# Column sums of four-tile arrays: one strided VectorE sum and one TensorE product in place of four products

## The chip, the core and the metric

The kernel runs on one core of a Trainium2 chip, as one program. The metric is the device time of one execution in microseconds (us). TensorE multiplies matrices, VectorE and ScalarE do elementwise work, SyncE issues the loads of the weights. On the profile's pages these are PE (matmul) and PEld (weight load), DVE, ACT and SP. TensorE's granted clock is given as a share of 2.4 GHz: 1.00 is 2.4 GHz and 0.50 is 1.2 GHz, the other of its two levels.

## What is computed

256 tokens of width 2048 run through two layers of a first block and one layer of a second, all in float32. Each layer normalizes its input, multiplies it by a wide input matrix, runs several mixers on slices of the result, normalizes each mixer's output over its channels, multiplies by an output matrix, and ends in a gated feed-forward part. What matters here are the norms over the 512 channels of a mixer, whose data stand with the channels on the partitions:

```python
# first block, in each of its two layers
hf = h.astype(jnp.float32)
mu = jnp.mean(hf, axis=-1, keepdims=True)
var = jnp.mean(jnp.square(hf - mu), axis=-1, keepdims=True)
hf = (hf - mu) * lax.rsqrt(var + EPS) * ln_g + ln_b
y_a = jax.nn.silu(hf)
...
y = jnp.concatenate([rms_normalize(y_a), rms_normalize(y_b), rms_normalize(y_c)], axis=-1)
# second block, in its one layer
y_b = rms_norm(rglru_mixer(...), grp_norm_w[l, 0])
y_d = rms_norm(short_conv_mixer(...), grp_norm_w[l, 2])
```

Ten of these sums over channels are touched: in each layer of the first block the mean and the variance of the convolution branch, the squares of `y_a` and the squares of `y_c` (the pooling branch); in the second block the squares of the LRU branch and of the short convolution.

## The kernel before

An array of 512 channels by 256 tokens stands as four tiles of 128 channels (partitions) by 256 tokens, side by side in a row of 1024 numbers per partition. `column_sums` sums it over all 512 channels: for each tile one product of the constant matrix `ones` (128x128, in the tile `C`) with the tile, the four accumulated in one PSUM bank, so that each of the 128 rows of the bank holds the sum. ScalarE then takes the root of the bank into `XL[:, 0, :]` (`root_of_sums`), VectorE takes its reciprocal into `XL[:, 1, :]` and multiplies all four tiles by it. `XL` has four rows of 256; row 2 isn't in use at these places.

The large products are cut into units of 1024 weights per partition. SyncE loads a unit into `WS`, ScalarE copies its rounded part to `WH` (L749), VectorE takes what is left into `WL` (`split`, L1320), and TensorE multiplies with both (L1858, which is the line of every plain product). All three tiles are rings of four. The work of the mixers is woven in by hand: in each loop over units `u`, each engine runs its split for unit `u + 4` and the part of `mixers_pe`, `mixers_act` or `mixers_dve` (`mixers2_...` in the second block) that is written for the number `u`. Tables such as `MEAN_AT, VAR_AT, RMS_AT = 57, 59, 62` and `POOL_RMS_AT = 80`, `LRU_RMS_AT = 21`, `SC_RMS_AT = 89` say at which unit. The order on an engine is therefore fixed when the program is built, and an instruction that waits holds up everything behind it on its engine.

At `u` TensorE first multiplies unit `u` and then does its part of the mixers. VectorE does its part of the mixers first and then the split of unit `u + 4` (except in the last unit of each eight in the first block's input part). The scores of attention head `h` (L1858, `SCR` 64x128 by 64x256, from `SCORES_AT`) go from TensorE to VectorE (L970, L973), then to ScalarE's exponential (L440), then back to TensorE, which transposes them (L1642).

Semaphores of the places: `s_cv` counts the steps of the convolution (124 per layer), `s_sqr` ScalarE's arrays of squares in the first block, `s_csq` those in the second, `s_col` and `s_csum` the finished column sums.

Of the kernel before, what the change touches and what calls it, by code (L numbers as in the profile page):

```python
# [9 lines left out]
ALU = mybir.AluOpType  # L10
ACT = mybir.ActivationFunctionType
AX = mybir.AxisListType.X
# [66 lines left out]
IN_ORDER = [0, 1, 2, 4, 6, 3, 5, 7, 8]  # L79
IN_BASE = [0, 4, 2, 0, 4, 0, 4, 0, 4]  # L80
TAPS = 31

# [33 lines left out]
def build(nc, a, out, stop=None):  # L118
    with ExitStack() as ctx:
# [67 lines left out]
        f3 = lambda t: t[:, 0:1024].rearrange("p (a b) -> p a b", a=4)  # L187
        flat = lambda v: v.rearrange("p a b -> p (a b)")
        junk = [T1[:, 0:1024], T2[:, :], T3[:, :], flat(XL[:, :, :])]
        row_scale = lambda n: PR[:, 192:192 + S] if n < 2 * DEPTH else flat(ROWS[:, :, :])  # L190
        by_row = lambda n: row_scale(n)[:, None, :].to_broadcast((P, 4, S))
        SCALED = [0, 2, 4, 5]
# [756 lines left out]
        def mixers_dve(dve, l, u):  # L949
# [8 lines left out]
            def y_low(kt, high, src):  # L958
# [2 lines left out]
                dve.scalar_tensor_tensor(out=XT[:, kt, 1, :], in0=src, scalar=col(G_MIX + kt), in1=XT[:, kt, 0, :].bitcast(F32),  # L961
                                         op0=ALU.mult, op1=ALU.subtract).then_inc(s_yt, 1)

            for h in heads_at(SCORES_AT, u):
                if h == 0:
                    dve.wait_ge(s_kc, 32 * (l + 1))
                dve.wait_ge(s_S, 16 * l + h + 1)
                if h >= 2:
                    dve.wait_ge(s_p, 16 * l + h - 1)
                dve.scalar_tensor_tensor(out=neg_s[:, h % 2, :], in0=PS[:, score_bank(h), :], scalar=-1.0,  # L970
                                         in1=KC[:, K_BIAS:K_BIAS + 2 * S], op0=ALU.mult, op1=ALU.subtract).then_inc(s_sb, 1)
                dve.wait_ge(s_sb, 16 * l + h + 1)
                dve.tensor_reduce(neg_max[:, 2 * (h % 2):2 * (h % 2) + 2],  # L973
                                  neg_s[:, h % 2, :].rearrange("p (t k) -> p t k", t=NT), AX, ALU.min).then_inc(s_nm, 1)
            for h in heads_at(OUTPUT_AT, u):
                if h % 4 == 3:
# [7 lines left out]
                    dst = y_b[:, :, 256 * g:256 * g + 256].rearrange("p t (h e) -> p h t e", e=64)  # L984
                    dve.tensor_tensor(dst, o, r[:, :, :, None].to_broadcast((P, 4, NT, 64)), ALU.mult).then_inc(s_yb, 1)
            if u == MEAN_AT:

                dve.wait_ge(s_cv, 4 * TAPS * (l + 1))
                dve.wait_ge(s_col, 4 * l + 1)
                for n in range(4):  # L990
                    ins = dve.scalar_tensor_tensor(out=acc[:, n, :], in0=PS[:, 7, 0:S], scalar=-1.0 / 512, in1=acc[:, n, :],
                                                   op0=ALU.mult, op1=ALU.add)
                ins.then_inc(s_lna, 1)
# [67 lines left out]
        def mixers2_dve(dve, u):  # L1061
# [56 lines left out]
            if u == LRU_SCAN_AT:  # L1118
# [5 lines left out]
                dve.wait_ge(s_lsq, 2)  # L1124
                dve.tensor_tensor(lru_xc, lru_xc, lru_gate, ALU.mult).then_inc(s_ly, 1)
            if u == LRU_RMS_AT:
                over_root(1, lru_xc, s_cn)

            if u in (DECAY_AT, DECAY_T_AT):
# [138 lines left out]
            if u == SC_OUT_AT:  # L1268
# [4 lines left out]
                low(4, sgu_yT, lambda i: col(G2_GRP + 4 + i))  # L1273
                low(8, gdn_yT, lambda i: col(G2_GDN))
            if u == SC_RMS_AT:
                over_root(2, sc_b, s_cn)
            if u == SC_SPLIT_AT:
                low(12, sc_b, lambda i: col(G2_GRP + 8 + i))
# [37 lines left out]
        def _(dve):  # L1316
# [96 lines left out]
            def conv(l, i0, i1):  # L1413

                for i in range(i0, i1):
                    j, n = divmod(i, 4)
                    if i == 0:
                        dve.wait_ge(s_glu, l + 1)
                    if j:
                        dve.wait_ge(s_cv, 4 * TAPS * l + i - 3)  # L1420
                    w = col(CONV_W + 4 * j + n)
                    if j == 0:
                        dve.tensor_scalar(acc[:, n, :], hpad[:, n, 0:S], w, col(CONV_B + n), ALU.mult, ALU.add).then_inc(s_cv, 1)
                    else:
                        dve.scalar_tensor_tensor(out=acc[:, n, :], in0=hpad[:, n, j:j + S], scalar=w, in1=acc[:, n, :],  # L1425
                                                 op0=ALU.mult, op1=ALU.add).then_inc(s_cv, 1)
# [139 lines left out]

        def mixers_pe(pe, mm, l, u):

            def column_sums(src, bank=7):

                for n in range(4):
                    last = mm(PS[:, bank, 0:S], ones, src[:, n, :], n == 0, n == 3)
                last.then_inc(s_col, 1)

            if u == POOL_AT:

# [4 lines left out]
                    last = mm(PS[:, 6 + n // 2, (n % 2) * S:(n % 2 + 1) * S], pw[:, n, :], pooled[:, n, :], True, True)  # L1581
                last.then_inc(s_mix, 1)
            if u == POOL_RMS_AT:
                pe.wait_ge(s_sqr, 3 * l + 3)
                column_sums(sq, 4)
            if u == MEAN_AT:
                pe.wait_ge(s_yb, 4 * l + 2)
                pe.wait_ge(s_cv, 4 * TAPS * (l + 1))
                column_sums(acc)
            if u == VAR_AT:  # L1590
                pe.wait_ge(s_sqr, 3 * l + 1)
                column_sums(sq)
            if u == RMS_AT:
                pe.wait_ge(s_std, 3 * l + 1)
                pe.wait_ge(s_sqr, 3 * l + 2)
                column_sums(sq)
            if u in TURN_QK_AT:
                i = TURN_QK_AT.index(u)
                half, src = i // 2, (q_nat, k_nat)[i % 2]
# [91 lines left out]

        def mixers2_pe(pe, mm, u):

            def column_sums(src):
                for n in range(4):
                    last = mm(PS[:, 6, 0:S], ones, src[:, n, :], n == 0, n == 3)
                last.then_inc(s_csum, 1)

            def each(bank, lhs, rhs, signal):
                for m in range(8):  # L1700
# [28 lines left out]
                last.then_inc(s_lm, 1)  # L1729
            if u == LRU_RMS_AT:  # L1730
                pe.wait_ge(s_lg, 2)
                pe.wait_ge(s_csq, 1)
                column_sums(f3(T1))

            if u == GCUM_AT:
                pe.wait_ge(s_g, 1)
# [108 lines left out]
                    last.then_inc(s_gyt, 1)  # L1845

            if u == SC_RMS_AT:
                pe.wait_ge(s_csq, 2)
                column_sums(sqs)

        @block.tensor
        def _(pe):
# [263 lines left out]
```

## Time and profile before

| | |
|---|---|
| median of 3 runs | 3406.37 us (3404.65 to 3410.67) |
| profiled execution | 3403.2 us, of which the span of the trace is 3401.4 us |
| TensorE matmul busy | 3332.5 us, 98% of the span |
| VectorE busy | 2014.0 us, 59% |
| ScalarE busy | 1656.9 us, 49% |
| mean granted clock | 0.995 |

The busy share of TensorE is near its limit nearly everywhere, so the page says at once which engine the others serve. It doesn't say which of TensorE's waits are short and which engine ends them: that is read from the timeline at each of the ten places. In the timeline a row gives start, duration, engine, line and operation; neighbouring equal instructions are merged into one row, and the idle time in brackets is that before the row's first instruction.

### The profile page before, as it was taken

Reading aid. Unit: us, or ns where it says so; the run is one execution under the profiler, and the core shown is the slowest. Engines: PE = TensorE matmul, PEld = TensorE weight load, DVE = VectorE, ACT = ScalarE, POOL = GpSimd, SP = SyncE. Lnnn points to the kernel's source line nnn. Section 1 sums busy time; section 2 is a strip of 40 time slices with the busy share of each in tenths; the row PEclk is TensorE's granted clock in tenths of the full one; section 3 lists DMA queues with packets and bytes.
Section 4 is the critical chain, followed back from the end, with each engine's and each line's share of the span. In section 5 each row is a group of like instructions: output and inputs, shape, how many; then the busy total and the mean of one; then the engine's idle time right before and its main releaser. Section 6 shows DMA issues by size and latency. Waiting matters only on the chain.

```text
span 3401.4 us, 45756 instructions
## 1 busy us (share of the span) xinstructions
PE 3332.5 (98%) x17107; PEld 2830.2 (83%) x17107; DVE 2014.0 (59%) x2443; ACT 1656.9 (49%) x2045; POOL 0.2 (0%) x4
## 2 busy tenths in 40 slices
PE   8999999999999999999999999988999999999998
PEld 8888788888888988888888888888898888888887
DVE  5866644544444786664454444568555777777544
ACT  4565544444344556454444444454544655566443
POOL 0000000000000000000000000000000000000000
PEclk9999999999999999999999999999999999999999
DMA  6644566666666654556666666544355556655654
GB/s 217 179 124 150 179 189 188 190 187 189 206 193 191 186 166 119 168 179 187 191 190 187 189 204 196 174 137 130 114 159 191 159 182 186 193 182 181 216 192 161
DMA packets 268619, 603.59 MB, mean 177 GB/s; under 512 B 22120, under 2 KB 24653, under 8 KB 268493
## 3 DMA queue, kind: packets, MB, share of 16 engines
q1 hardware_dynamic: 261165, 592.32, 56.9%
q10 hardware_dynamic: 7328, 9.51, 0.9%
q8 instruction: 89, 1.46, 0.2%
q14 instruction: 37, 0.30, 0.0%
HBM read 599.66 MB, written 2.10 MB: 177 GB/s over the span
## 4 chain that ended last, share of the span: by engine, by line
PE 94%; DVE 3%; ACT 2%; issue 1%; ACTq 0%; DMA 0%; SPq 0%; DVEq 0%
PE PS L1858 92%; PE PS L1663 1%; PE PS L1642 1%; DVE WL L1320 0%; DVE x L1398 0%; ACT WH L749 0%; DVE T L1162 0%; PE PS L1960 0%; DVE SCR L1381 0%; PE PS L1609 0%; DVE SCR L1116 0%; DVE XT L1340 0%; ACT XT L771 0%; DMA WS<-in_w_in_dram 0%; DVE SCR L1057 0%
## 5 line engine op out<-in xcount | busy, mean ns | idle before, releaser
L1320 DVE TENSOR_TENSOR WL<-WS,WH 128x1024 fp32r<-128x1024 f32 x1120 | 1364.8, 1224 | 1187.5 <-ACT WH L749 1186.9
L749 ACT ACTIVATE WH<-WS 128x1024 fp32r<-128x1024 f32 x1120 | 1176.6, 1059 | 1499.7 <-PE PS L1858 1450.6
L1858 PE MATMUL PS<-WH,XT 128*128 128x512 f32 x4544 | 1400.7, 392 | 7.3 <-DVE XT L961 3.0
L1858 PEld LDWEIGHTS PS<-WH,XT 128*128 128x128 f32 x4544 | 853.4, 188 | 185.8 <-DVE WL L1320 4.4
L1858 PE MATMUL PS<-WL,XT 128*128 128x512 f32 x2272 | 856.0, 390 | 0.0
L1858 PE MATMUL PS<-XT,WH 128*128 128x256 f32 (+1 forms) x3200 | 832.2, 337 | 15.9 <-DVE XT L1340 8.5
L1858 PE MATMUL PS<-XT,WL 128*128 128x256 f32 x2304 | 651.3, 283 | 0.0
L1858 PEld LDWEIGHTS PS<-XT,WH 128*128 128x128 f32 x3200 | 548.4, 192 | 84.8 <-issue 14.2
L1858 PE MATMUL PS<-WH,HT 128*128 128x512 f32 x2112 | 568.0, 389 | 0.0
L1858 PEld LDWEIGHTS PS<-WL,XT 128*128 128x128 f32 x2272 | 427.4, 188 | 86.4
L1858 PEld LDWEIGHTS PS<-WH,HT 128*128 128x128 f32 x2112 | 396.2, 188 | 82.0
L1858 PEld LDWEIGHTS PS<-XT,WL 128*128 128x128 f32 x2304 | 440.5, 191 | 0.0
L1858 PE MATMUL PS<-WL,HT 128*128 128x512 f32 x1056 | 327.2, 389 | 0.0
L1858 PEld LDWEIGHTS PS<-WL,HT 128*128 128x128 f32 x1056 | 198.3, 188 | 41.2
L1858 PE MATMUL PS<-SCR 128*128 128x64 f32 (+6 forms) x712 | 117.1, 308 | 11.0 <-DVE SCR L1163 6.4
L1858 PEld LDWEIGHTS PS<-SCR 128*128 128x128 f32 (+3 forms) x712 | 95.6, 188 | 30.5 <-issue 24.1
L1302 DVE SCALAR_TENSOR_TENSOR T<-T,C 128x256 f32<-128x256 f32 x176 | 73.5, 481 | 48.2 <-ACT T L733 48.2
L1425 DVE SCALAR_TENSOR_TENSOR SCR<-SCR,PR 128x256 f32<-128x256 f32 x240 | 101.7, 479 | 0.0
L733 ACT ACTIVATE T<-T,C 128x256 f32<-128x256 f32 x88 | 45.8, 591 | 68.7 <-DVE T L1296 68.7
L771 ACT ACTIVATE XT<-PS,PR 128x256 fp32r<-128x256 f32 x96 | 37.0, 483 | 29.6 <-PE PS L1960 29.6
L1340 DVE SCALAR_TENSOR_TENSOR XT<-PS,PR,XT 128x256 fp32r<-128x256 f32 x96 | 39.7, 478 | 9.1 <-ACT XT L771 9.1
L1960 PE MATMUL PS<-C,x 128*128 128x128 f32 x192 | 28.9, 289 | 14.4 <-POOLq L1564 7.3
(266 smaller groups left out, 1145.5 us busy)
## 6 DMA issues: line engine op xcount, KB each, us to landing
WS<-in_w_in_dram SPq DMA_DIRECT2D x232, 512.0 KB, 3.7
WS<-in_w_gate_dram SPq DMA_DIRECT2D x176, 512.0 KB, 3.7
WS<-in_w_up_dram SPq DMA_DIRECT2D x176, 512.0 KB, 3.7
WS<-in_w_down_dram SPq DMA_DIRECT2D x176, 512.0 KB, 3.7
WS<-in_ffn_up_dram SPq DMA_DIRECT2D x176, 512.0 KB, 4.5
WS<-in_w_out_dram SPq DMA_DIRECT2D x96, 512.0 KB, 4.0
WS<-in_ffn_down_dram SPq DMA_DIRECT2D x88, 512.0 KB, 4.3
x<-in_x_dram SPq DMA_DIRECT2D x4, 512.0 KB, 5.7
```

The lines of the kernel that those rows point to most:

```text
L733: ins = act.activation(f3(dst)[:, n, :], ffn_pad[:, n, 2:2 + S], ACT.Identity, scale=conv_j[:, 2, g, n:n + 1], bias=conv_j[:, 3, g, n:n + 1])
L749: act.activation(WH[:, i % RING, :], WS[:, i % RING, :], ACT.Copy).then_inc(s_hi, 1)
L771: act.activation(XT[:, kt, 0, :], PS[:, kt // 2, (kt % 2) * S:(kt % 2 + 1) * S], ACT.Copy, scale=col(g + kt)).then_inc(s_xh, 1)
L1302: ins = dve.scalar_tensor_tensor(out=f3(dst)[:, n, :], in0=ffn_pad[:, n, k:k + S], scalar=conv_j[:, k, g, n:n + 1], in1=f3(dst)[:, n, :], ...
L1320: dve.tensor_tensor(WL[:, i % RING, :], WS[:, i % RING, :], WH[:, i % RING, :].bitcast(F32), ALU.subtract).then_inc(s_lo, 1)
L1340: dve.scalar_tensor_tensor(out=XT[:, kt, 1, :], in0=PS[:, kt // 2, (kt % 2) * S:(kt % 2 + 1) * S], scalar=col(g + kt), in1=XT[:, kt, 0, :] ...
L1425: dve.scalar_tensor_tensor(out=acc[:, n, :], in0=hpad[:, n, j:j + S], scalar=w, in1=acc[:, n, :], op0=ALU.mult, op1=ALU.add).then_inc(s_cv, 1)
L1642: last = pe.transpose(PS[:, 6, k * S + t * P:k * S + (t + 1) * P], prob[:, h % 2, t * S + k * P:t * S + (k + 1) * P], ident)
L1663: last = pe.transpose(quad(6)[:, n, t * P:(t + 1) * P], h[:, t, n * P:(n + 1) * P], ident)
L1858: return pe.matmul(o, w, r, start=start, stop=stop, skip_group_check=True)
L1960: last = pe.transpose(PS[:, kt // 2, (kt % 2) * S + t * P:(kt % 2) * S + (t + 1) * P], x[:, t, kt * P:(kt + 1) * P], ident)
```

## The change

`column_sums` becomes one product of `ones` with a tile `tile_sum` (128x256, row 2 of `XL`). `tile_sum` is written ahead of it by a new VectorE instruction, `tensor_reduce` over the view `over_tiles(...)`, in which the tile index is innermost: for each token it adds four numbers that stand 256 numbers apart. Each TensorE wait now counts the VectorE sum too. For the mean, the reduction is one more step of `s_cv` (`CONV_STEPS = 125` per layer), for the others one more step of `s_sqr` or `s_csq`.

```diff
+CONV_STEPS = 4 * TAPS + 1
...
+        tile_sum = XL[:, 2, :]
+        over_tiles = lambda v: v.rearrange("p a b -> p b a")
...
+            for k, at in enumerate((VAR_AT, RMS_AT, POOL_RMS_AT - 1)):
+                if u == at:
+                    dve.wait_ge(s_sqr, 6 * l + 2 * k + 1)
+                    dve.wait_ge(s_col, 4 * l + k + 1)
+                    dve.tensor_reduce(tile_sum, over_tiles(sq), AX, ALU.add).then_inc(s_sqr, 1)
             for h in heads_at(SCORES_AT, u):
...
             if u == MEAN_AT:
-
-                dve.wait_ge(s_cv, 4 * TAPS * (l + 1))
+                dve.wait_ge(s_cv, CONV_STEPS * l + 4 * TAPS)
+                dve.tensor_reduce(tile_sum, over_tiles(acc), AX, ALU.add).then_inc(s_cv, 1)
+            if u == MEAN_AT:
+
+                dve.wait_ge(s_cv, CONV_STEPS * (l + 1))
...
             if u == LRU_RMS_AT:
+                dve.wait_ge(s_csq, 1)
+                dve.tensor_reduce(tile_sum, over_tiles(f3(T1)), AX, ALU.add).then_inc(s_csq, 1)
                 over_root(1, lru_xc, s_cn)
...
             if u == SC_RMS_AT:
+                dve.wait_ge(s_csq, 3)
+                dve.tensor_reduce(tile_sum, over_tiles(sqs), AX, ALU.add).then_inc(s_csq, 1)
                 over_root(2, sc_b, s_cn)
...
-            def column_sums(src, bank=7):
-
-                for n in range(4):
-                    last = mm(PS[:, bank, 0:S], ones, src[:, n, :], n == 0, n == 3)
-                last.then_inc(s_col, 1)
+            def column_sums(bank=7):
+
+                mm(PS[:, bank, 0:S], ones, tile_sum, True, True).then_inc(s_col, 1)
...
             if u == RMS_AT:
                 pe.wait_ge(s_std, 3 * l + 1)
-                pe.wait_ge(s_sqr, 3 * l + 2)
-                column_sums(sq)
+                pe.wait_ge(s_sqr, 6 * l + 4)
+                column_sums()
```

Nothing changes its place on any engine; ten instructions come in on VectorE and thirty products go on TensorE. Where the new ones stand decides what TensorE waits for. VectorE at the sums of the variance (u = 59) and of the squares of `y_a` (u = 62) in the first layer; `WL<-WS,WH` is a split, `XL<-XL` and `SCR<-SCR,XL` are the reciprocal and the multiplication of the variance, `SCR<-PS,SCR` and `SM<-SCR` the scores of head 8. Before:

```order
L1320 TENSOR_TENSOR WL<-WS,WH 128x1024 [waits s_hi] x2
L954 RECIPROCAL XL<-XL 128x256 [waits s_std,s_lna]
L956 TENSOR_TENSOR SCR<-SCR,XL 128x1024 [waits s_rstd]
L1320 TENSOR_TENSOR WL<-WS,WH 128x1024 [waits s_hi] x2
L970 SCALAR_TENSOR_TENSOR SCR<-PS,SCR 128x512 [waits s_p,s_S]
L973 TENSOR_REDUCE SM<-SCR 128x2 [waits s_sb]
```

And now:

```order
L1335 TENSOR_TENSOR WL<-WS,WH 128x1024 [waits s_hi]
L971 TENSOR_REDUCE XL<-T 128x256 [waits s_col,s_sqr]
L1335 TENSOR_TENSOR WL<-WS,WH 128x1024 [waits s_hi]
L957 RECIPROCAL XL<-XL 128x256 [waits s_std,s_lna]
L959 TENSOR_TENSOR SCR<-SCR,XL 128x1024 [waits s_rstd]
L1335 TENSOR_TENSOR WL<-WS,WH 128x1024 [waits s_hi] x2
L971 TENSOR_REDUCE XL<-T 128x256 [waits s_col,s_sqr]
L978 SCALAR_TENSOR_TENSOR SCR<-PS,SCR 128x512 [waits s_p,s_S]
L981 TENSOR_REDUCE SM<-SCR 128x2 [waits s_sb]
```

The sum for the variance stands between the splits of units 62 and 63, the one for the squares behind the splits of units 64 and 65. TensorE at the second of these places, before:

```order
L1858 MATMUL PS<-WH,XT 128x512
L1858 MATMUL PS<-T,C 128x256 [waits s_sqr,s_std]
L1858 MATMUL PS<-T,C 128x256 x3
L1858 MATMUL PS<-SCR 128x256 [waits s_sb,s_qk]
L1858 MATMUL PS<-SCR 128x256
L1858 MATMUL PS<-WH,XT 128x512 [waits s_lo]
```

And now:

```order
L1869 MATMUL PS<-WH,XT 128x512
L1869 MATMUL PS<-XL,C 128x256 [waits s_sqr,s_std]
L1869 MATMUL PS<-SCR 128x256 [waits s_sb,s_qk]
L1869 MATMUL PS<-SCR 128x256
L1869 MATMUL PS<-WH,XT 128x512 [waits s_lo]
```

Four products have become one, in the same place; behind it stand the scores of head 8 and unit 63. VectorE in the second block at the LRU's sum (u = 21), where `SCR<-SCR` is the LRU's gate and the last two rows are the reciprocal and the multiplication by it. Now:

```order
L1136 TENSOR_TENSOR SCR<-SCR 128x1024 [waits s2_lsqrt,s2_dve_chain]
L1335 TENSOR_TENSOR WL<-WS,WH 128x1024 [waits s_hi] x3
L1139 TENSOR_REDUCE XL<-T 128x256 [waits s2_csq]
L1082 RECIPROCAL XL<-XL 128x256 [waits s2_croot]
L1083 TENSOR_TENSOR SCR<-SCR,XL 128x1024 [waits s2_dve_chain]
```

Three splits (units 22 to 24) stand between the gate and the new sum; before, the same rows stood there without the sum.

## Rows read from the trace of the kernel before

**Rows 1.** The page: busy time by engine, and the chain that ended last.

```profile
PE 3332.5 (98%) x17107; PEld 2830.2 (83%) x17107; DVE 2014.0 (59%) x2443; ACT 1656.9 (49%) x2045; POOL 0.2 (0%) x4
...
PE 94%; DVE 3%; ACT 2%; issue 1%; ACTq 0%; DMA 0%; SPq 0%; DVEq 0%
```

**Rows 2.** Groups by form, TensorE: line, operation, out<-in, shapes, count | busy us, mean ns.

```profile
L1858 PE MATMUL PS<-T,C 128*128 128x256 f32 x56 | 13.3, 380 | 1.2 <-ACT T L594 1.2
```

**Rows 3.** Groups by form, VectorE: reductions.

```profile
L1221 DVE TENSOR_REDUCE SM<-SCR 128x8 f32<-128x1024 f32 x1 | 1.2, 1220 | 0.0
...
L1087 DVE TENSOR_REDUCE T<-PS 128x16 f32<-128x64 f32 x1 | 0.2, 218 | 0.0
```

**Rows 4.** Timeline, first layer, the sum of the pooling branch (u = 80).

```profile
300.52 1.06 ACT L502 ACTIVATE T<-SCR 128x1024 f32<-128x1024 f32 x1
...
302.80 1.23 DVE L1320 TENSOR_TENSOR WL<-WS,WH 128x1024 fp32r<-128x1024 f32 x1 [3.24 <-ACT WH L749]
...
304.18 1.89 PE L1858 MATMUL PS<-T,C 128*128 128x256 f32 x8
...
305.72 0.81 PE L1858 MATMUL PS<-WH,XT 128*128 128x512 f32 x2
```

**Rows 5.** Timeline, first layer, the sum for the mean (u = 57).

```profile
203.88 1.27 DVE L1425 SCALAR_TENSOR_TENSOR SCR<-SCR,PR 128x256 f32<-128x256 f32 x3
...
205.30 1.97 PE L1858 MATMUL PS<-SCR,C 128*128 128x256 f32 x8
...
206.91 0.58 PE L1858 MATMUL PS<-WH,XT 128*128 128x512 f32 x1
```

**Rows 6.** Timeline, first layer, the sum for the variance (u = 59).

```profile
211.20 1.23 DVE L1320 TENSOR_TENSOR WL<-WS,WH 128x1024 fp32r<-128x1024 f32 x1
...
212.57 1.89 PE L1858 MATMUL PS<-T,C 128*128 128x256 f32 x8
```

**Rows 7.** Timeline, first layer, the sum of the squares of `y_a` (u = 62).

```profile
223.40 1.89 PE L1858 MATMUL PS<-T,C 128*128 128x256 f32 x8
...
224.82 1.23 DVE L1320 TENSOR_TENSOR WL<-WS,WH 128x1024 fp32r<-128x1024 f32 x1 [5.21 <-ACT WH L749]
...
226.39 0.69 DVE L970 SCALAR_TENSOR_TENSOR SCR<-PS,SCR 128x512 f32<-128x512 f32 x1 [0.34 <-PE PS L1858]
```

**Rows 8.** Timeline, second block, the LRU's sum (u = 21).

```profile
2285.32 1.06 ACT L594 ACTIVATE T<-SCR 128x1024 f32<-128x1024 f32 x1 [1.82 <-DVE SCR L1125]
...
2286.53 1.97 PE L1858 MATMUL PS<-T,C 128*128 128x256 f32 x8 [1.17 <-ACT T L594]
...
2287.83 1.23 DVE L1320 TENSOR_TENSOR WL<-WS,WH 128x1024 fp32r<-128x1024 f32 x1 [0.27 <-ACT WH L749]
```

**Rows 9.** Timeline, second block, the short convolution's sum (u = 89).

```profile
2559.06 2.35 DVE L1320 TENSOR_TENSOR WL<-WS,WH 128x1024 fp32r<-128x1024 f32 x2
...
2560.91 1.89 PE L1858 MATMUL PS<-SCR,C 128*128 128x256 f32 x8
```

**Rows 10.** The chain that ended last, in order of time: start, us, what.

```profile
288.70 77.23 PE PS L1858 x340
...
2286.53 32.76 PE PS L1858 x266
...
2554.62 35.39 PE PS L1858 x150
```

**Rows 11.** Timeline: two of TensorE's waits.

```profile
236.94 1.11 PE L1642 MATMUL PS<-C,SCR 128*128 128x128 f32 x4 [2.06 <-ACT SCR L440]
...
2254.13 2.47 PE L1858 MATMUL PS<-SCR 128*128 128x256 f32 x5 [4.66 <-issue]
```

**Rows 12.** Stretches: length, then busy us (instructions) of PE, PEld, DVE, ACT, POOL, granted clock, DMA share, GB/s.

```profile
235.00:240.00 5.00, 3.06 (x15) 3.06 (x16) 4.90 (x7) 2.64 (x6) 0.00 (x0) 0.66 0.38 108
1325.00:1330.00 5.00, 2.94 (x25) 2.83 (x25) 4.90 (x6) 2.57 (x7) 0.00 (x0) 1.00 0.34 105
2255.00:2260.00 5.00, 5.00 (x22) 4.23 (x22) 1.30 (x2) 0.61 (x2) 0.00 (x0) 0.78 0.65 206
```

More of the change, by code:

```diff
@@ L1419, in conv @@
                     if j:
-                        dve.wait_ge(s_cv, 4 * TAPS * l + i - 3)
+                        dve.wait_ge(s_cv, CONV_STEPS * l + i - 3)
                     w = col(CONV_W + 4 * j + n)
@@ L1583, in mixers_pe @@
             if u == POOL_RMS_AT:
-                pe.wait_ge(s_sqr, 3 * l + 3)
-                column_sums(sq, 4)
+                pe.wait_ge(s_sqr, 6 * l + 6)
+                column_sums(4)
             if u == MEAN_AT:
                 pe.wait_ge(s_yb, 4 * l + 2)
-                pe.wait_ge(s_cv, 4 * TAPS * (l + 1))
-                column_sums(acc)
+                pe.wait_ge(s_cv, CONV_STEPS * (l + 1))
+                column_sums()
             if u == VAR_AT:
-                pe.wait_ge(s_sqr, 3 * l + 1)
-                column_sums(sq)
+                pe.wait_ge(s_sqr, 6 * l + 2)
+                column_sums()
             if u == RMS_AT:
                 pe.wait_ge(s_std, 3 * l + 1)
-                pe.wait_ge(s_sqr, 3 * l + 2)
-                column_sums(sq)
+                pe.wait_ge(s_sqr, 6 * l + 4)
+                column_sums()
             if u in TURN_QK_AT:
@@ L1692, in mixers2_pe, with column_sums @@
         def mixers2_pe(pe, mm, u):
[L1694 to L1697, printed above, removed]
+            def column_sums():
+                mm(PS[:, 6, 0:S], ones, tile_sum, True, True).then_inc(s_csum, 1)
             def each(bank, lhs, rhs, signal):
@@ L1731, in mixers2_pe @@
                 pe.wait_ge(s_lg, 2)
-                pe.wait_ge(s_csq, 1)
-                column_sums(f3(T1))
+                pe.wait_ge(s_csq, 2)
+                column_sums()
             if u == GCUM_AT:
@@ L1847, in mixers2_pe @@
             if u == SC_RMS_AT:
-                pe.wait_ge(s_csq, 2)
-                column_sums(sqs)
+                pe.wait_ge(s_csq, 4)
+                column_sums()
         @block.tensor
```

## The prediction

> **What bounds the kernel now.** I read the page first, for who is the limit, then the chain that ended last, for where TensorE's own time counts, then the timeline at each of the ten sums, for what TensorE would find there if it had to wait for VectorE. The page says that TensorE is busy 98% of the span and stands for 94% of the chain [rows 1]. VectorE is busy 59%, so another ten sums of about a microsecond are no load on it. What counts is when each is done. The chain runs through TensorE without a break at the pooling sum, at the LRU's sum and at the short convolution's [rows 10]. A microsecond less of TensorE there is a microsecond less of time, and a microsecond of waiting is a microsecond more.
>
> **What the change removes.** Each product of `ones` with a tile is two records in the trace: 56 records with a tile of `T` [rows 2] for 28 products, that is seven sums. At the pooling sum 8 records last 1.89 us, one lasts 0.38, so records start (1.89 - 0.38) / 7 = 0.216 us apart. From the first of them to the next large product it is 305.72 - 304.18 = 1.54 us [rows 4]; where TensorE stood idle ahead of them it is 206.91 - 205.30 = 1.61 us [rows 5], since the first weights could not be loaded early. Three of four products are six records, 6 x 0.216 = **1.30 us** for each sum. Ten sums make 13.0 us, 0.38% of the time, if nothing is waited for. What is left takes 1.54 - 1.30 = 0.24 us, or 0.31 after an idle stretch.
>
> **What a VectorE sum costs.** A reduction of 1024 contiguous numbers in SBUF to 8 takes 1.22 us [rows 3]. The new one reads as many, but neighbours in its order lie 1024 bytes apart, and it writes 256 results. The nearest row is the reduction of 64 numbers in PSUM with a step of 32 bytes, 0.218 us [rows 3]. Between the two rows lie 960 numbers and 1.002 us, 1.04 ns for each: per number the strided one costs no more than the contiguous. Below 1.22 us I see nothing. The upper bound is that each number costs twice as much, 1.22 + 1024 x 1.04 ns = 2.29 us. I take 1.22, since the strided row is the one that it is nearest to. From the end of an operation to TensorE's start it was 2286.53 - (2285.32 + 1.06) = 0.15 us [rows 8], and I allow 0.03 between two operations of VectorE. So TensorE's sum can begin 0.03 + 1.22 + 0.15 = **1.40 us** after VectorE's preceding work ends, or after the squares are done if these are later.
>
> A sentence of the Trainium skill speaks against that price: the page "SBUF — State Buffer", in the part of "Door 1: The DMA port swizzle" on cachelines, says that each access that crosses to a new 16-byte line pays a penalty. Each read here does so. The page gives no size for the penalty, and no row of this trace shows an SBUF read with such a step. It is weighed as the second rival below.
>
> **Place by place**, each against TensorE's start of before.
>
> - *Pooling, twice.* The new sum stands ahead of the split at 302.80, for which VectorE had waited 3.24 us. The squares end at 300.52 + 1.06 = 301.58, the sum at 302.83, TensorE could start at 302.98 and gets there only at 304.18 [rows 4]. 1.2 us are in hand: the whole of -1.30. The split moves back by a few hundredths, and is for a unit that comes three units later.
> - *Mean, twice.* The last steps of the convolution end at 203.88 + 1.27 = 205.15 and TensorE starts at 205.30 [rows 5]: it already waits for VectorE. Now it starts at 205.15 + 1.40 = 206.55 and is through at 206.86, against 206.91: **-0.05**. VectorE's next work waited for that sum anyway.
> - *Variance, twice.* The split of unit 62 ends at 211.20 + 1.23 = 212.43, so TensorE starts at 213.83 instead of 212.57 [rows 6] and is through at 214.14, against 212.57 + 1.54 = 214.11: **+0.03**.
> - *Squares of `y_a`, twice.* Here VectorE's order costs most. Ahead of the new sum stands the split of unit 65. VectorE had been idle for 5.21 us, but in front of this split: it waits for ScalarE's copy, which comes late. The split runs from 224.82 to 226.05 [rows 7], long after TensorE's sum of before began at 223.40. Now TensorE starts at 227.45, 4.05 us later, and gets back 1.30; without early weights 0.07 more are lost: **+2.82**. Behind the wait stand the scores of head 8, which VectorE (L970 at 226.39), ScalarE and the splits behind them wait for. So the delay goes into the chain, not beside it.
> - *LRU, once.* Three splits stand ahead, the last from 2287.83 to 2289.06. TensorE starts at 2290.46 instead of 2286.53 [rows 8]: 3.93 - 1.30 = **+2.63**. Then 32.76 us of TensorE's chain follow without a wait [rows 10], and nothing takes it back.
> - *Short convolution, once.* Two splits end at 2559.06 + 2.35 = 2561.41, TensorE starts at 2562.81 instead of 2560.91 [rows 9]: 1.90 - 1.30 + 0.07 = **+0.67**.
>
> Sum: 2 x (-1.30 - 0.05 + 0.03 + 2.82) + 2.63 + 0.67 = **+6.3 us**. Where the sum is fully hidden it gains 2.6 us in all; at three places in the program's order it gives that back more than twice.
>
> **The clock.** After the wait of 2.06 us at 236.94 [rows 11] the stretch from 235 to 240 has a granted clock of 0.66, after the same wait in the second layer 1.00 [rows 12]. Behind the wait of 4.66 us [rows 11] it is 0.78 [rows 12]. So a wait of 2 us may bring the lower level, and a longer one is likelier to. 0.66 over 5 us is (1 - 0.66) x 5 = 1.7 us of lost work. The LRU's new wait, about 5 us with the 1.17 that were there, stands ahead of TensorE work that is all on the chain: I add 1.7. The one at `y_a`'s squares, about 3.9 us, has the 2.06 us wait behind it two units later, in which a slower stretch is mostly lost anyway: I add nothing, and keep 2 x 1.7 for the range. Together **+8.0 us**.
>
> Worked against the profiled execution, 3403.2 us (span 3401.4), that is 3411.2. The three runs have their median 3.2 us above it, so I predict 3406.4 + 8.0 = **3414 us**, +0.23%. For this kernel some 0.2%, 6.8 us, is what can be told from no change.
>
> **The rivals.**
>
> 1. *The forecast*, VectorE's order makes TensorE wait at three kinds of places: +4 to +12 us, 3410 to 3418. Chance 0.55.
> 2. *Strided reads cost double*, the rule above as a mechanism of this kernel: each new sum takes 2.29 us. At the pooling sums the 1.2 us in hand just cover the 1.07 more. At the other eight it is all waited for: 8 x 1.07 = 8.6 us more, 3423 us. For it speaks that no row shows the step; against it the row of 64 numbers [rows 3]. Chance 0.12.
> 3. *The delays are taken back later.* The delay at `y_a`'s squares could be swallowed by the 2.06 us wait behind it, if that wait ended on something that does not hang on head 8's scores. Then 4.1 us less and no slower stretch at the LRU: +6.3 - 4.1 = +2 us, 3409, no measurable change. Against it: the wait ends on ScalarE's exponential of head 9, behind ScalarE's work for head 8. Chance 0.27.
> 4. *Faster*: the sums lie under TensorE's work at all ten places, as at the pooling sum, and 13.0 us go, 3393 us. It decides at the splits ahead of the sums: they would have to end before 223.40 - 1.40 = 222.0 at `y_a`'s squares instead of 226.05, and before 2285.1 at the LRU instead of 2289.06. VectorE's order is fixed, and the split at 224.82 waits for ScalarE. If only these two waits were half as long, the sum would be near zero. Chance 0.06.
>
> **The numbers.** The forecast's range is widened down to the third case and up to half of what the second adds: 3408 to 3422 us. Of the first case about 0.05 and of the second most lie outside, as does the fourth. Slower by over 0.2%: most of case 1 on the upper side of 3413.2, and case 2, 0.57. Within 0.2%: the rest of case 1 and case 3, 0.37. Faster: 0.06.
>
> **What would show it.** In the trace of the changed kernel: at `y_a`'s squares one product, two records, in front of which TensorE stood idle for about 3.9 us with VectorE as the releaser, and about 5 us at the LRU, 1.7 at the short convolution and 1.3 at the mean; no wait at the pooling sums, and 1.3 us less between the large products there. The new reductions should last 1.22 us; 2.3 would be the second rival. The scores of head 8 should be 2.8 us later against the sum for the variance. The forecast is wrong if the split of unit 65 runs earlier than at 224.82 [rows 7] for some reason, if the wait at 236.94 shrinks by the delay, or if the clock reacts to the new waits in more places than one.

## The result, and the profile after

The changed kernel takes 3425.36 us (median of 7 runs, 3413.22 to 3428.05) against 3406.37 us of the kernel before (7 runs): a ratio of 1.0058, with a 95% interval of 1.0042 to 1.0073. It is slower by 19 us. The prediction had the sign and said 3414 us; the time lies above its range of 3408 to 3422.

The page of the kernel after, busy time and chain, answers to [rows 1]:

```profile
span 3426.3 us, 45652 instructions
...
PE 3341.3 (98%) x17047; PEld 2833.0 (83%) x17047; DVE 2033.2 (59%) x2453; ACT 1658.4 (48%) x2045; POOL 0.2 (0%) x4
...
PE 93%; DVE 4%; ACT 2%; issue 1%; ACTq 0%; SPq 0%; DMA 0%; DVEq 0%
```

TensorE has 60 records fewer and is busy 8.8 us longer: a part of what it still does, it does at a lower clock. The run's mean granted clock is 0.988, before it was 0.995. VectorE's share of the chain went from 3% to 4%.

The new sums among the groups by form, VectorE, of the kernel after. L996 is the sum for the mean, L971 those for the variance, the squares of `y_a` and the pooling branch, L1139 the LRU's and L1290 the short convolution's:

```profile
L971 DVE TENSOR_REDUCE XL<-T 128x256 f32<-128x1024 f32 x6 | 11.6, 1935 | 4.1 <-ACT T L505 4.1
L996 DVE TENSOR_REDUCE XL<-SCR 128x256 f32<-128x1024 f32 x2 | 3.8, 1908 | 0.1
L1290 DVE TENSOR_REDUCE XL<-SCR 128x256 f32<-128x1024 f32 x1 | 1.9, 1906 | 0.0
L1139 DVE TENSOR_REDUCE XL<-T 128x256 f32<-128x1024 f32 x1 | 1.9, 1878 | 0.0
```

Each takes about 1.91 us, not the 1.22 us of [rows 3].

TensorE's waits, by what ended them (us in total, times, longest):

```profile
PE PS L1869 <- DVE XL L971: 12.0, 4, 4.4
...
PE PS L1869 <- DVE XL L1139: 4.2, 1, 4.2
PE PS L1869 <- DVE XL L996: 4.1, 2, 2.1
PE PS L1869 <- DVE XL L1290: 2.2, 1, 2.2
```

Eight waits for the new sums, 22.5 us. The two pooling sums are not among them. The timeline of the kernel after at the places of [rows 5, 6, 7, 4, 8, 9], in this order:

```profile
206.13 0.67 PE L1869 MATMUL PS<-XL,C 128*128 128x256 f32 x2 [2.05 <-DVE XL L996]
...
213.87 0.70 PE L1869 MATMUL PS<-XL,C 128*128 128x256 f32 x2 [1.59 <-DVE XL L971]
...
224.95 1.23 DVE L1335 TENSOR_TENSOR WL<-WS,WH 128x1024 fp32r<-128x1024 f32 x1 [5.21 <-ACT WH L752]
...
226.10 1.88 DVE L971 TENSOR_REDUCE XL<-T 128x256 f32<-128x1024 f32 x1
...
228.12 0.89 PE L1869 MATMUL PS<-XL,C 128*128 128x256 f32 x2 [4.44 <-DVE XL L971]
228.95 2.07 PE L1869 MATMUL PS<-SCR 64*128 64x256 f32 x4
...
231.06 0.69 DVE L978 SCALAR_TENSOR_TENSOR SCR<-PS,SCR 128x512 f32<-128x512 f32 x1 [3.08 <-PE PS L1869]
...
241.61 0.66 PE L1655 MATMUL PS<-C,SCR 128*128 128x128 f32 x4
...
307.50 0.60 PE L1869 MATMUL PS<-XL,C 128*128 128x256 f32 x2
307.75 0.58 PE L1869 MATMUL PS<-WH,XT 128*128 128x512 f32 x1
...
2305.26 1.19 PE L1869 MATMUL PS<-XL,C 128*128 128x256 f32 x2 [4.20 <-DVE XL L1139]
...
2585.73 0.70 PE L1869 MATMUL PS<-XL,C 128*128 128x256 f32 x2 [2.22 <-DVE XL L1290]
```

At `y_a`'s squares the order of events is the one forecast: the split, late by ScalarE's copy, then the new sum, then TensorE's product. At the pooling sum nothing is waited for, and from the product to the next large one it is 0.25 us instead of 1.54.

The granted clock in some 5 us stretches of the kernel after (it stands third from the end of a row). The one from 1305 is behind the mean's sum of the second layer, the one from 1325 behind that layer's squares, the one from 2305 behind the LRU's sum:

```profile
230.00:235.00 5.00, 5.00 (x13) 3.48 (x12) 2.51 (x3) 2.47 (x6) 0.00 (x0) 0.50 0.08 7
235.00:240.00 5.00, 5.00 (x34) 4.19 (x33) 2.08 (x3) 4.47 (x7) 0.00 (x0) 0.97 0.28 97
1305.00:1310.00 5.00, 5.00 (x19) 3.81 (x17) 3.45 (x9) 2.02 (x2) 0.00 (x0) 0.80 0.36 105
1325.00:1330.00 5.00, 4.03 (x8) 2.48 (x9) 1.59 (x3) 0.02 (x1) 0.00 (x0) 0.50 0.38 105
2305.00:2310.00 5.00, 4.74 (x20) 4.59 (x21) 3.08 (x4) 0.47 (x1) 0.00 (x0) 0.50 0.71 268
```

0.50 is the lower of the two levels, 1.2 GHz. TensorE is busy for the whole of 230 to 235 and gets through 13 records, because each takes twice as long.

**Where the time is.** I set the same TensorE instructions of both profiled executions beside each other. The spans differ by 24.9 us, more than the medians do. From the mean's sum to the output projection it is 4.4 us more in the first layer and 7.9 in the second; the stage around the LRU's sum (2265 to 2341 us before) has 8.0 more, that around the short convolution's 2.8. The two pooling stages have 1.3 less each. The other 4.3 us are in stretches that the change does not touch, feed-forward parts above all, in steps of about 1.5 us: one fall of the clock more in one execution than in the other. A second profiled execution of the changed kernel (the first experiment below) shows which of these figures repeat. The four stages have 6.6, 7.4, 8.0 and 2.8 us more there, the pooling stages again 1.3 less each. Three of the 1.5 us steps (at 1110, 1463 and 2200 us before) are not there; two (at 375 and 2250) are, but each of them also stands in a kernel below in which TensorE waits for no new sum. So what the stages have is the change's, to some 2 us each, and those steps are chance. The four stages and the two of pooling are called the touched stages below: 21 us more in the first execution, 22 in the second.

One difference of another kind runs through the profiled executions. The feed-forward part of the second block, which has no new sum, takes 8.6 to 8.7 us less in three of the fourteen (the waits filled, the gain alone, the early additions) than in the other eleven, at a granted clock of 1.00 in both. The kernel before, then the one with the waits filled, the instructions of PE in brackets:

```profile
2800.00:2900.00 100.00, 100.00 (x567) 86.75 (x566) 75.12 (x104) 59.18 (x66) 0.00 (x0) 1.00 0.60 186
...
2800.00:2900.00 100.00, 100.00 (x579) 88.19 (x578) 73.83 (x105) 60.21 (x69) 0.00 (x0) 1.00 0.59 183
```

The cause is not known. The runs without a profile don't say of which kind they are, so a median over a few of them can be off by a part of these 8.7 us; single runs of the kernel before lie between 3394.6 and 3411.2 us.

### The profile page after: what moved, and what is told of

Its sections match the earlier page's. It is cut to its first block, busy times and chain, and to the rows that moved or that the text cites. A ratio compares the mean times of both kernels' runs of the same rounds, so it can differ in the third digit from the quotient of the medians.

```text
span 3426.3 us, 45652 instructions
## 1 busy us (share of the span) xinstructions
PE 3341.3 (98%) x17047; PEld 2833.0 (83%) x17047; DVE 2033.2 (59%) x2453; ACT 1658.4 (48%) x2045; POOL 0.2 (0%) x4
## 4 chain that ended last, share of the span: by engine, by line
PE 93%; DVE 4%; ACT 2%; issue 1%; ACTq 0%; SPq 0%; DMA 0%; DVEq 0%
PE PS L1869 91%; DVE WL L1335 1%; PE PS L1676 1%; ACT WH L752 1%; PE PS L1655 1%; DVE x L1413 0%; DVE T L1175 0%; PE PS L1971 0%; DVE SCR L1396 0%; DVE XL L971 0%; DVE SCR L1127 0%; DVE XT L1355 0%; ACT XT L774 0%; DVE SCR L1440 0%; DMA WS<-in_w_in_dram 0%
## 5 line engine op out<-in xcount | busy, mean ns | idle before, releaser
L443 ACT ACTIVATE SCR<-SCR,SM 128x256 f32<-128x256 f32 x64 | 32.2, 504 | 24.0 <-DVE SM L981 24.0
```

What stands on the lines that cost most here:

```text
L443: ins = act.activation(prob[:, h % 2, t * S:(t + 1) * S], neg_s[:, h % 2, t * S:(t + 1) * S], ACT.Exp, bias=neg_max[:, 2 * (h % 2) + t:2 * ...
```

## The experiments

Three groups of four kernels were run, each group beside runs of the kernel before (its medians there 3404.85, 3405.96 and 3402.30 us). A ratio is to the kernel before in the same group, with its 95% interval. The changed kernel, run again in the second group, gave 1.0055 [1.0037, 1.0072] (3423.38 us), so the result repeats.

> The changed kernel once more, beside the other experiments. Single runs of one kernel spread over 13 to 17 us, so the size of the effect needs more of them. Theory A and rival alike: 3420 to 3427 us, 16 to 22 above the kernel before. If it comes out below 3415, a part of the 19 us first measured was chance.

### Contiguous numbers

```diff
-        over_tiles = lambda v: v.rearrange("p a b -> p b a")
+        over_tiles = lambda v: flat(v).rearrange("p (b a) -> p b a", a=4)
```

Each result is now the sum of four neighbouring numbers in place of one number from each channel tile, so this kernel leaves out the sum over the channel tiles; counts, results and order stay.

> As the changed kernel, but each VectorE sum adds four neighbouring numbers instead of four that stand 1024 bytes apart (so it sums other numbers; count, destination and waits are the same). Theory A, the stride is what made a sum 1.9 us instead of 1.22: the ten sums last 1.22 us here, TensorE waits 0.69 us less at eight places, and the time is some 5.5 us below the changed kernel's 3425, about 3420, or lower still if shorter waits leave the clock at 2.4 GHz more often. Rival, the 256 results that it writes are what costs: the sums stay at 1.9 us and the time at 3425.

Measured: 1.0012 [1.0001, 1.0023]. The groups by form of this kernel, VectorE:

```profile
L971 DVE TENSOR_REDUCE XL<-T 128x256 f32<-128x1024 f32 x6 | 7.3, 1214 | 4.1 <-ACT T L505 4.1
L996 DVE TENSOR_REDUCE XL<-SCR 128x256 f32<-128x1024 f32 x2 | 2.4, 1220 | 0.1
```

As many numbers in and results out, and 1.21 us in place of 1.91. So the stride of the reads costs 0.69 us, and writing 256 results costs nothing visible. Eight sums that are waited for make 8 x 0.69 = 5.5 us. The time fell by 1.0055 - 1.0012 = 0.43%, or 15 us, though, with an uncertainty of some 7, where 5.5 or somewhat more were expected. In the profiled execution the touched stages take 9 to 10 us less than in those of the changed kernel. So shorter waits brought more than their length; how much more isn't shown.

### The gain alone

```diff
-                mm(PS[:, bank, 0:S], ones, tile_sum, True, True).then_inc(s_col, 1)
+                mm(PS[:, bank, 0:S], ones, src[:, 0, :], True, True).then_inc(s_col, 1)
```

This is the kernel before, with no VectorE sums and one product in place of four: it leaves out three quarters of every sum.

> The kernel before with one product per sum, over the first channel tile alone, and no VectorE sum: it leaves out three quarters of each sum. This is the gain of the change without its cost. Both theories: 30 products less at 0.43 us each are 13.0 us, 3393 us, 0.4% below the kernel before. Rival: TensorE's fp32 products of this size are partly hidden, and less than half of it shows (over 3399).

Measured: 0.9948 [0.9934, 0.9962], 17.7 us less by the ratio and 16.5 by the medians. The trace says more than this number. From the large product ahead of each of the ten sums to the one behind it TensorE needs 1.29 or 1.30 us less at nine places and 1.26 at the LRU's (without what a fall of the clock ahead of it costs), 13 us in all, as forecast. The median's surplus isn't explained by the sums: this profiled execution is one of the three with the quicker feed-forward part, and if more of these six runs than of those before were of that kind, some of the 17 us come from there. TensorE's timeline at head 9, and before it VectorE's read of head 8's scores, this kernel:

```profile
223.26 0.68 DVE L970 SCALAR_TENSOR_TENSOR SCR<-PS,SCR 128x512 f32<-128x512 f32 x1
...
233.81 1.11 PE L1640 MATMUL PS<-C,SCR 128*128 128x128 f32 x4 [3.20 <-ACT SCR L440]
```

The wait of 2.06 us in [rows 11] has grown to 3.20. Head 8's scores are done at 222.11, but VectorE reads them only at 223.26, behind its late split, and from that read to the row above it is 10.55 us. Of the 1.30 us gained at the squares in each layer 1.15 are lost to that split again.

### The waits filled

```diff
+            def fill(n, bank=7):
+                for _ in range(n):
+                    mm(PS[:, bank, 0:S], ones, C[:, 0:S], True, True)
...
+                fill(4)
...
+                pe.wait_ge(s_lna, 3 * l + 1)
+                fill(3)
...
+                fill(9)
```

The calls shown stand ahead of the waits at the mean, the variance (with a wait for VectorE, which has to have read the mean's bank) and the squares; there are nine products at the LRU's and four at the short convolution's sum too. It is the changed kernel, but TensorE makes products that nobody reads in place of standing idle. VectorE, and so the moment at which each sum is ready, stays.

> The changed kernel with idle products of the constants (4 at the mean, 3 at the variance, 9 at the squares, 9 at the LRU, 4 at the short convolution) put on TensorE ahead of each wait for VectorE, into the bank that the sum then overwrites. They fill 1.3 to 3.9 us of waits of 1.6 to 4.4 us. Theory A, the clock falls to 1.2 GHz behind the new waits and that costs most of the 19 us: with TensorE kept at work the time falls by 8 to 13 us to 3412 to 3417, and the granted clock rises from 0.988 to 0.992 or more. Rival B, the waits alone cost the time and the clock falls in stretches that were idle anyway: no change, 3422 to 3428.

Measured: 1.0027 [1.0014, 1.0040]. Its timeline around the squares, first layer:

```profile
224.46 4.05 PE L1883 MATMUL PS<-C 128*128 128x256 f32 x18
...
228.99 0.70 PE L1883 MATMUL PS<-XL,C 128*128 128x256 f32 x2 [0.47 <-DVE XL L971]
229.61 1.13 PE L1883 MATMUL PS<-SCR 64*128 64x256 f32 x4
...
230.78 0.69 DVE L978 SCALAR_TENSOR_TENSOR SCR<-PS,SCR 128x512 f32<-128x512 f32 x1 [1.85 <-PE PS L1883]
...
241.34 0.66 PE L1663 MATMUL PS<-C,SCR 128*128 128x128 f32 x4 [2.10 <-ACT SCR L443]
```

And its stretches behind the squares of both layers and behind the LRU's sum, which TensorE begins at 2298.17 here:

```profile
230.00:235.00 5.00, 5.00 (x23) 3.50 (x22) 2.51 (x3) 2.74 (x6) 0.00 (x0) 1.00 0.13 29
1325.00:1330.00 5.00, 5.00 (x29) 3.95 (x29) 1.89 (x3) 4.13 (x7) 0.00 (x0) 1.00 0.35 102
2300.00:2305.00 5.00, 5.00 (x45) 5.00 (x44) 4.80 (x5) 1.21 (x3) 0.00 (x0) 1.00 0.40 124
2305.00:2310.00 5.00, 5.00 (x45) 5.00 (x44) 2.67 (x8) 3.71 (x4) 0.00 (x0) 1.00 0.56 200
```

With the waits full of work the granted clock behind them stays at 1.00, the scores take 1.13 us and not 2.07, and half of the loss is gone: 1.0055 or 1.0058 to 1.0027, some 10 us, with an uncertainty of some 6. The profiled executions agree: the touched stages take 11 us more than before here, against 21 and 22. The other half, 9 us with an interval of 5 to 14, is the waiting as such.

### The sums moved ahead of the splits

```diff
-            for k, at in enumerate((VAR_AT, RMS_AT, POOL_RMS_AT - 1)):
+            for k, at in enumerate((VAR_AT, RMS_AT - 1, POOL_RMS_AT - 1)):
...
-            if u == LRU_RMS_AT:
+            if u == LRU_RMS_AT - 2:
...
-            if u == SC_RMS_AT:
+            if u == SC_RMS_AT - 1:
```

Strided sums as in the changed kernel, for the squares, the LRU and the short convolution written one, two and one unit earlier in VectorE's order.

> The changed kernel with three of its VectorE sums moved ahead of splits in VectorE's order: the squares' sum ahead of the split of unit 65, the LRU's ahead of the splits of units 23 and 24, the short convolution's ahead of the split of unit 92. Theory A (order and clock): TensorE's waits there fall from 4.4, 4.2 and 2.2 us to about 1.2, 2.1 and 1.8, which is 5 us by the waits alone (the wait behind head 9 comes back), and the clock falls less often, 5 us more: 3413 to 3417. Rival B (waits alone): 3420. Rival C (the order doesn't matter since the delayed splits hold TensorE up instead): 3425.

Measured: 0.9991 [0.9980, 1.0002], 22 to 23 us less than the changed kernel by the ratios, where the most hopeful expectation had 8 to 12: all three were too high. Its timeline around the squares:

```profile
222.60 1.97 DVE L971 TENSOR_REDUCE XL<-T 128x256 f32<-128x1024 f32 x1 [2.75 <-ACT T L481]
...
224.72 0.67 PE L1871 MATMUL PS<-XL,C 128*128 128x256 f32 x2 [0.92 <-DVE XL L971]
225.07 1.23 DVE L1337 TENSOR_TENSOR WL<-WS,WH 128x1024 fp32r<-128x1024 f32 x1 [0.50 <-ACT WH L752]
225.32 1.13 PE L1871 MATMUL PS<-SCR 64*128 64x256 f32 x4
...
226.48 0.69 DVE L978 SCALAR_TENSOR_TENSOR SCR<-PS,SCR 128x512 f32<-128x512 f32 x1 [0.19 <-PE PS L1871]
...
237.03 0.66 PE L1657 MATMUL PS<-C,SCR 128*128 128x128 f32 x4 [2.07 <-ACT SCR L443]
```

The sum now fills VectorE's idle time ahead of the late split, and that split starts at 225.07, 0.12 us later than it did. TensorE's wait fell from 4.44 to 0.92 us. VectorE does exactly the same work as in the changed kernel: its place in the order was the fault.

### Two contiguous additions, in the old and in the early places

```diff
-                    dve.tensor_reduce(tile_sum, over_tiles(sq), AX, ALU.add).then_inc(s_sqr, 1)
+                    sum_tiles(dve, sq).then_inc(s_sqr, 1)
...
+        def sum_tiles(dve, src):
+            dve_chain[0] += 1
+            dve.tensor_tensor(XL[:, 2:4, :], src[:, 0:2, :], src[:, 2:4, :], ALU.add).then_inc(s_dc, 1)
+            dve.wait_ge(s_dc, dve_chain[0])
+            return dve.tensor_tensor(tile_sum, tile_sum, XL[:, 3, :], ALU.add)
```

The whole computation, as two additions of contiguous tiles (0.69 and 0.42 us) in place of one strided sum. First in the places of the change:

> The changed kernel with each strided sum replaced by two contiguous VectorE additions, two tiles onto two (128x512), then one onto one (128x256), in the same places. By the rows of this kernel's own additions they should last 0.69 and 0.43 us, 1.14 with the step between, where the strided sum lasts 1.91. Theory A (price and clock): as with contiguous reads, waits 0.77 us shorter at eight places, 3408 to 3414 us. Rival (what helped there was chance): 3420 to 3427.

Measured: 1.0025 [1.0013, 1.0038]; TensorE waits 1.30 us at the mean, 0.82 at the variance, 3.70 at the squares, 4.91 at the LRU and 1.42 at the short convolution. That is about as in the kernel with contiguous numbers, and the intervals of the two overlap. Then with the three sums early, as above:

> Both mends: two contiguous additions, and at the squares, the LRU and the short convolution they stand ahead of the splits. Theory A: waits of TensorE of about 1.3 at the mean, 0.8 at the variance, 0.3 at the squares, 2.4 at the LRU, 0.6 at the short convolution. By the waits 5 us below the kernel with early strided sums (3403), 3397 to 3400, which is 0.15 to 0.2% below the kernel before. Rival: the gain at the squares is swallowed by the wait for head 9's exponential behind it, and the rest is chance of the clock: 3401 to 3404.

Measured: 0.9989 [0.9977, 1.0002], 3401.26 us, where the rival expectation stood. The wait at the squares is gone and that for head 9 is 2.58 us. This is the whole version with the lowest ratio; it can't be told from the kernel before with certainty, nor from the one with early strided sums.

### The load on VectorE alone

```diff
+            for k, at in enumerate((VAR_AT, RMS_AT, POOL_RMS_AT - 1)):
+                if u == at:
+                    dve.wait_ge(s_sqr, 3 * l + k + 1)
+                    dve_chain[0] += 1
+                    dve.tensor_reduce(tile_sum, over_tiles(sq), AX, ALU.add).then_inc(s_dc, 1)
+                    dve.wait_ge(s_dc, dve_chain[0])
```

This is an edit of the kernel before, with like instructions at the mean and the short convolution. TensorE's four products as before; VectorE makes nine of the ten strided sums (all but the LRU's) and nobody reads them.

> The kernel before, with its four products, and beside them nine of the ten strided VectorE sums (all but the LRU's), whose result nobody reads and for which TensorE doesn't wait. Theory A: VectorE's load costs nothing by itself; only at the squares the sum (1.9 us, behind the split of unit 65) holds up the scores of head 8, by some 1.6 us in each layer: 3406 to 3409 us. Rival: VectorE's extra 17 us are what slows the kernel, through later splits: over 3415.

Measured: 1.0009 [0.9996, 1.0021]. 9 x 1.9 = 17 us of VectorE's time cost 3 us at most likely and 7 at most, and the expectation had about these 3 for the scores of head 8, which stand behind the sum of the squares. Load is not the cause.

### One place at a time

Only the squares' sum early (the first hunk of the early version):

> The changed kernel with only the squares' sum moved ahead of the split of unit 65 (two places, one in each layer). All three moves together brought 21 us. Theory A: the squares' wait of 4.4 us is where most of it went, by the wait (3.5 us less, of which 2.1 come back as the wait for head 9: 1.4 in each layer) and by the clock that falls behind it: 3406 to 3411 us. Rival: the LRU's and the short convolution's places carry as much: 3413 to 3418.

Measured: 1.0018 [1.0006, 1.0031]. Only the LRU's sum early:

> The changed kernel with only the LRU's sum moved ahead of the splits of units 23 and 24 (one place). Theory A: the wait falls from 4.3 to 3.1 us and stays long enough for the clock to fall: 1 to 3 us less, 3420 to 3423. Rival: the LRU carries a third of the 21 us: 3416 to 3418.

Measured: 1.0053 [1.0039, 1.0067], though TensorE's wait there fell to 1.71 us, and the stage around it from 84.4 us to 78.7 in the profiled execution. Then the squares' wait filled alone, with these products in both layers and nowhere else:

```diff
+                fill(9)
```

> The changed kernel with nine idle products (3.9 us) ahead of TensorE's wait at the squares, in both layers, and nowhere else. The wait for VectorE lasts as long as before. Filling all waits brought about 10 us. Theory A: the clock behind the squares' wait carries half or more of that: 3414 to 3419 us, and the granted clock after the squares' sum is 1.00. Rival: what the clock costs there is taken back by the wait for head 9 behind it (which vanished in the changed kernel and returns when it is filled), so filling brings 0 to 3 us: 3421 to 3424.

Measured: 1.0050 [1.0036, 1.0064], between the two expectations. By the ratios the early sum at the squares is worth about 13 us of the 20, the filling there about 2, the early one at the LRU about 1, with +-5 us on each. By the stages of the profiled executions the early sum at the squares is worth 6 to 7, the early one at the LRU 6 and the filling 2 to 3. Two things stand between the two ways of counting. This group's median of the kernel before is 2.5 to 4 us lower than that of the others; against the medians of the changed kernel itself, the early LRU's sum takes 3 to 5 us less. And chance in the clock is large: up to the second block, the kernel with the squares' sum early and the one with all three early are the same program, and their two stages there have 6.7 and 0.8 us more than before. So these runs show that both places count, and not how much each does.

Last, a mixture: one product with two additions at the pooling sums, at the squares and at the short convolution, the last two early; the four products of before at the mean, the variance and the LRU.

```diff
+            def four_sums(src, bank=7):
+                for n in range(4):
+                    last = mm(PS[:, bank, 0:S], ones, src[:, n, :], n == 0, n == 3)
+                last.then_inc(s_col, 1)
...
-                column_sums()
+                four_sums(acc)
...
-                column_sums()
+                four_sums(sq)
```

> VectorE sums (two contiguous additions) only where TensorE hardly waits for them: at the pooling branch, and ahead of the splits at the squares and the short convolution. At the mean, the variance and the LRU TensorE does its four products as before. Theory A: -1.3 in each layer at the pooling sums, almost nothing at the squares (head 9's wait takes it back), -0.7 at the short convolution, and no new wait over 0.5 us: 3399 to 3402 us, 0.1% below the kernel before. Rival: the additions early in VectorE's order cost splits and so TensorE's time: 3405 or more.

Measured: 0.9994 [0.9983, 1.0006], 3402.79 us and not the 3399 to 3402 expected, no better than the early version. Fewer new waits did not help further, as far as these intervals can tell.

## Why the prediction was right in kind and wrong in size

**The gain, 13.0 us: held.** In the trace of the kernel with the gain alone each of the ten sums takes 1.26 to 1.30 us less, 13 us in all. At the pooling sums of the changed kernel it is 1.29 each too. The time fell by more, 16.5 to 17.7 us with an interval of 13 to 22, and what is over isn't shown to come from the sums.

**The places: held.** All eight waits stand where the prediction put them, none at the pooling sums. At the mean, squares, LRU and short convolution they were to be about 1.3, 3.9, 5 and 1.7 us; they are 2.05, 4.44, 4.20 and 2.22. What VectorE's order costs was shown by moving three sums in it: the whole loss went.

**The price of a VectorE sum: failed.** The prediction took 1.22 us, "since the strided row is the one that it is nearest to". That row was 64 numbers in PSUM [rows 3], and it says nothing on 1024 numbers in SBUF with a step of 1024 bytes. Nor does the line through the two rows show that a strided number costs no more: with two rows of different kinds and sizes, the 1.04 ns for each number is assumed for both. The sum measured 1.91 us, inside the bound of 2.29. It is 8 x 0.69 = 5.5 us, and the second rival, with 8.6, was right in kind and two thirds right in size. The Trainium skill's page "SBUF — State Buffer", in "Door 1: The DMA port swizzle", says that every access to a new 16-byte line pays; the kernel with contiguous numbers agrees, since there four neighbours share such a line and the price is gone.

**The clock, +1.7 us: failed, by the most.** The forecast's waits with the true price make 6.3 + 5.5 = 11.8 us; the kernel with filled waits, where the clock stays up behind them, measured 9 (5 to 14). The changed kernel measured 19 to 20 by the ratios. So the clock costs about 8 to 10 us, and the prediction had 1.7. It allowed one fall, at the LRU, and named the opposite as a risk ("if the clock reacts to the new waits in more places than one"). It did so behind both squares, behind the mean's wait of 2.05 us in the second layer (0.80 in the stretch from 1305, 1.6 us lost; in the second execution behind the mean's in both layers), behind the LRU's and, shorter, at the short convolution (1.6 us lost). With the price mended and the clock as it was, the sum is 3406.4 + 11.8 + 1.7 = 3420 us, inside the range. With contiguous numbers, where the price is the forecast one, the measured 1.0012 is 0 to 8 us, the whole forecast at its upper end. Its profiled execution has 12 us more than before in the touched stages, so that agreement may be in part chance.

**The lower clock behind the squares: failed in a reason.** The prediction let it cost nothing, because a wait of 2.06 us follows in which a slower stretch "is mostly lost anyway". But that wait does not end on TensorE's next work; it hangs on head 8's scores. From VectorE's read of those scores to head 9's transposes it is 236.94 - 226.39 = 10.55 us before [rows 7, 11], 241.61 - 231.06 = 10.55 after, 241.34 - 230.78 = 10.56 with filled waits, 237.03 - 226.48 = 10.55 with early sums, and 10.55 in the kernel with the gain alone. The chain through VectorE and ScalarE is the same length in all five, whether TensorE waits at its end or not. From the product to that read it is 1.79 us at the full clock and 2.94 at the lower one. So the slow scores cost 1.15 us in the first layer. In the second it is 3.23 us from the product to the read, and TensorE comes 0.28 late for the transposes besides: 1.7 us. The read in the first layer comes 4.67 us later than before, 0.13 of which was there ahead of the squares: 4.5 us for 2.82, that is 2.82 + 0.69 + 1.15 with 0.1 too much in the allowances. The rest of the reason held. TensorE falls back by 2 us more in the unit behind the scores, and gets these 2 us back because the wait of 2.06 us is gone. What was wrong was to let the scores themselves, which a chain hangs on, go in with that.

**The third rival, delays taken back later: refuted** by the same 10.55 us. The wait for head 9 did vanish in the changed kernel, which looks like the new delay taken back. What it took back is only the slow unit behind the scores; the delay of the chain stays.

**The LRU, forecast 2.63 and 1.7: too low.** Its stage has 8.0 us more in the profile. The wait has 2.63 + 0.69 = 3.3 of them, and the lower clock directly behind it 2.1. (TensorE also loses 1.45 us to a lower clock ahead of the sum, but the wait for VectorE swallows that.) Another 1.0 comes from a lower clock some 35 us behind the sum. All six executions with that sum late and its wait not filled have it. With the strided sum early (alone or with the other two) it is not there, with the early additions it is. The last 1.5, at the stage's end, stand in twelve of the thirteen other executions against this one of before, the kernel without any sum on VectorE too: they are not the change's. The prediction's 1.7 was nearly right for the stretch that it looked at; it had nothing for the later one. The time itself doesn't show this well: with this sum early the median fell by 1 us by the ratios and by 3 to 5 against the changed kernel's own medians, where the profile says 6.

**The fourth rival, faster: refuted as the kernel stands**, and its condition was right. It asked for sums that end before the splits ahead of them. With that order the time is that of before, not 3393: waits of 2.05 and 1.58 us at the mean and the variance and 3.13 at the LRU stay.

**Open:** how the 20 us divide between waiting and clock more closely than about half and half; what each place is worth by itself; which falls of the clock are chance; and what makes the second block's feed-forward part 8.7 us quicker in some executions.

## What to carry to other kernels

Work moved off the busiest engine is only a gain where the other engine delivers in time: look up what stands ahead of the new instruction in that engine's order, above all an instruction that itself waits, and put the new one ahead of it. Price a strided read by a row with that stride in that memory, or take the upper bound. A new wait of TensorE ahead of work that a serial chain hangs on costs its length and can cost the clock behind it too; fill it with idle products to see which half is which.

## What the runs showed of the hardware that I had not expected

- A reduction of 1024 fp32 numbers per partition in SBUF to 256 took 1.91 us with a step of 1024 bytes and 1.21 us with neighbours, a factor of 1.6, and two contiguous additions that do the same took 0.69 + 0.42 us.
- A granted clock of 0.50 stood behind waits of 4.2 and 4.4 us, and of 0.66 behind one of 2.06 us in one layer, with 1.00 behind the same wait in the other [rows 11, 12]. Products that nobody reads held it at 1.00 in the stretches behind the filled waits.
- Single runs of one kernel lie up to 17 us apart. Half of that can come from one place: in three of fourteen profiled executions TensorE got through 579 instructions in 100 us of the second block's feed-forward part, in the others through 567 or 568, at a granted clock of 1.00 in both, which makes 8.7 us. Falls of the clock at chance places, 1.5 us each, come on top.
